# A decoder block's conv norm: the first pair of statistics in split parts in blocks two to four

## The chip, the core and the metric

The kernel runs on one core of a Trainium2 chip. Times are microseconds (us) of device time for one execution of the whole program. The engines of the core are PE (TensorE: matmuls), PEld (its weight load), DVE (VectorE), ACT (ScalarE), POOL (GpSimd) and SP (SyncE, which issues DMAs). Each has its own queue of instructions, executes it in order, and waits on semaphores where it needs another engine's result.

## The reference, cut to what matters

One layer over 2048 tokens of 1024 features: a norm, one input projection, a gated linear attention over half of the columns and a convolution over the other half, an output projection, an MLP, and a last norm. The change is in the norm that follows the convolution:

```python
def channel_group_norm(u, g, b):
    B, S, C = u.shape                                   # C = 512, CONV_GROUPS = 8
    uf = u.astype(jnp.float32).reshape(B, S, CONV_GROUPS, C // CONV_GROUPS)
    mu = jnp.mean(uf, axis=-1, keepdims=True)
    var = jnp.mean(jnp.square(uf - mu), axis=-1, keepdims=True)
    y = ((uf - mu) * lax.rsqrt(var + EPS)).reshape(B, S, C)
    return (y * g.astype(jnp.float32) + b.astype(jnp.float32)).astype(u.dtype)
...
        u = c_in * jax.nn.sigmoid(c_gate)
        u = causal_depthwise_conv(u, conv_w[l], conv_b[l])
        o_conv = jax.nn.silu(channel_group_norm(u, conv_norm_g[l], conv_norm_b[l]))
        mixed = jnp.concatenate([o_gla, o_conv], axis=-1)
        h = h + jnp.einsum('bse,ed->bsd', mixed, w_out[l])
```

## The kernel before

The tokens go through the mixer in four blocks of 512 (`b` = 0 to 3 in the code, blocks 1 to 4 in this text), up to about 700 us of the span; the MLP fills the rest. In a block, the channels of the convolution are four tiles of 128 channels by 512 tokens, `j` = 0 to 3, held in `y_sb`. They are normed in two pairs. The products of the block are made of three fp32r matmuls each, high and low parts of both operands (`three_products`, lines 83 to 85 by their place: L83, L84, L85); twelve such matmuls are one unit of weights.

**The norm's statistics are matmuls.** A 128x128 matrix with 1/64 in two squares, `mean_grp`, averages over the channels of a group. For the second pair (`j` = 2, 3) the operand is split: ACT rounds it to an fp32r high part, `mix_hi` (L1614 for the mean, L1605 for the squares), POOL subtracts it from the operand for the low part, `mix_lo` (L1168 and L1178; DVE in block 4), and PE adds two fp32r matmuls, L2270 on the high part and L2271 on the low part. For the first pair (`j` = 0, 1) PE multiplies the fp32 operand itself: L2585 for the mean, on `y_sb`, and L2595 for the variance, on the squares in `res_sb`. The trace shows each such fp32 matmul as two records, so a pair is one row of four. `mix_hi` and `mix_lo` can't serve the first pair, since they still hold the operands of the block's output projection at that time.

**The steps of the norm** are, for a pair: `cn_mean` (PE the means; DVE takes them from `y_sb`, L2215; ACT squares into `res_sb`, L1603), `cn_var` (PE the variances, ACT their logarithm, L1618), `cn_rstd` (ACT Exp, L1623, POOL the product with `y_sb`, L1183) and, later, `cn_silu` and `cn_mixed` (ACT L1627, and the parts for the output projection, ACT L1636 and POOL L1187).

**What stands around them.** A step `g` is a column of the gate's projection, one or two units of PE (L83 to L85) and ACT's `silu_g` (L1549). The attention works in chunks of 128 tokens: `gla_expo` (DVE L2174 to L2176, then ACT L1567 to L1569 for `fac`), `gla_factors` (POOL: `k_end`, `q_in`, `qk`, L1044 to L1046), `gla_decayed` (POOL: `ke` and `qe` for seven levels, L1158 and L1159), `gla_heads` (ACT copies `qe` into `qe_head`, L1579), `gla_scores` (PE L2617 and L2624 on `qe_head` and `ke`, L2635, L2638), `gla_select` (DVE takes the levels from the scores into `probs`, L2054, L2064) and `gla_out`. `gn_mixed` is POOL's share of the norm of the attention's result of the block before (L1196, L1199), after ACT's `mix_hi` (L1663). `gate` is a small product for the decays (PE L2494, DVE `cum`).

**What sets the order** is one table, `ORDER`, of steps with their block. Each engine walks the whole table and issues its own share of each step in that order:

```python
        def run(do):
            for b, *step in ORDER:
                do(step, b)
```

So a step's place in the table sets its place in all five queues at once; the semaphores alone say how far one engine runs ahead of another. Nothing is reordered later.

## Time and profile before

| | us |
|---|---|
| median of 3 runs | 2025.48 (2025.23 to 2025.58) |
| the profiled execution, its own time | 2025.3 |
| its span | 2023.6 |
| PE busy | 2001.7 (99%) |
| DVE busy | 1474.7 (73%) |
| ACT busy | 957.9 (47%) |
| POOL busy | 443.5 (22%) |

The profile is of one execution; 1.7 us of its time lie outside the span. "Busy" is time in which an engine executes; for PE the ends of matmuls are modelled and overlap the next one's start, so PE's pace is read from the distance of starts. A wait belongs to the instruction that stands at the head of its engine's queue, and the name behind the arrow is the one that ended last by the profile.

### The profile page before, as it was taken

Reading aid. Unit: us, or ns where it says so; the run is one execution under the profiler, and the core shown is the slowest. Engines: PE = TensorE matmul, PEld = TensorE weight load, DVE = VectorE, ACT = ScalarE, POOL = GpSimd, SP = SyncE. Lnnn points to the kernel's source line nnn. Section 1 sums busy time; section 2 is a strip of 40 time slices with the busy share of each in tenths; the row PEclk is TensorE's granted clock in tenths of the full one; section 3 lists DMA queues with packets and bytes.
Section 4 is the critical chain, followed back from the end, with each engine's and each line's share of the span. In section 5 each row is a group of like instructions: output and inputs, shape, how many; then the busy total and the mean of one; then the engine's idle time right before and its main releaser. Section 6 shows DMA issues by size and latency. Waiting matters only on the chain.

```text
span 2023.6 us, 27171 instructions
## 1 busy us (share of the span) xinstructions
PE 2001.7 (99%) x9898; PEld 1636.7 (81%) x9898; DVE 1474.7 (73%) x2178; ACT 957.9 (47%) x1362; POOL 443.5 (22%) x593
## 2 busy tenths in 40 slices
PE   8999999999999999999999999999999999999998
PEld 7787778787878778888888888888888888888887
DVE  3899978887878978877789777777664646545475
ACT  4456664355244563565657554555232333323253
POOL 5543475235126441000000000000020201202031
PEclk9999999999999999999999999999999999999999
DMA  6885458455565555444446433335977567565674
GB/s 229 284 282 158 135 204 295 165 170 183 198 202 198 175 204 194 161 146 141 146 165 210 151 121 124 130 119 193 371 238 265 191 203 262 181 220 186 206 240 176
DMA packets 175268, 395.76 MB, mean 196 GB/s; under 512 B 15424, under 2 KB 64672, under 8 KB 174624
## 3 DMA queue, kind: packets, MB, share of 16 engines
q1 hardware_dynamic: 154688, 317.47, 46.4%
q10 hardware_dynamic: 20448, 76.56, 10.9%
q8 instruction: 79, 1.29, 0.3%
q14 instruction: 53, 0.43, 0.1%
HBM read 301.70 MB, written 92.27 MB: 195 GB/s over the span
## 4 chain that ended last, share of the span: by engine, by line
PE 59%; DVE 0%; issue 0%; POOLq 0%; ACT 0%; POOL 0%; ACTq 0%
PE acc L83 20%; PE acc L85 19%; PE acc L84 19%; PE acc L2331 0%; DVE rows_b L2023 0%; DVE rows_b L2005 0%; DVE f_tile L1895 0%; DVE part_t L1891 0%; DVE ring_sum L1868 0%; POOLq L260 0%; ACT m_junk L1465 0%; POOL m_rstd L1117 0%; ACTq L1470 0%
## 5 line engine op out<-in xcount | busy, mean ns | idle before, releaser
L1985 DVE TENSOR_TENSOR down_lo<-down_raw,down_hi 128x1536 fp32r<-128x1536 f32 x112 | 200.5, 1790 | 229.8 <-ACT down_hi L1440 229.8
L83 PE MATMUL acc<-down_hi 128*128 128x512 f32 x896 | 348.5, 389 | 0.0
L84 PE MATMUL acc<-down_lo,down_hi 128*128 128x512 f32 x896 | 348.5, 389 | 0.0
L85 PE MATMUL acc<-down_hi,down_lo 128*128 128x512 f32 x896 | 348.5, 389 | 0.0
L1440 ACT ACTIVATE down_hi<-down_raw 128x1536 fp32r<-128x1536 f32 x112 | 166.7, 1488 | 360.8 <-PE acc L85 188.9
L1723 DVE SCALAR_TENSOR_TENSOR acc<-u_sb,cw_col,acc 128x512 f32<-128x512 f32 x464 | 313.0, 748 | 0.3
L1354 ACT ACTIVATE ring_hi<-ring_sum 128x512 fp32r<-128x512 f32 x155 | 97.8, 631 | 251.3 <-DVE ring_sum L1868 248.8
L83 PE MATMUL acc<-xT_hi,wt 128*128 128x512 f32 x512 | 204.1, 399 | 1.8 <-DVE u_sb L2088 1.0
L1099 POOL TENSOR_TENSOR rows_a<-rows_a,second 128x512 f32<-128x512 f32 x20 | 25.3, 1300 | 803.5 <-ACT second L1448 655.5
L85 PE MATMUL acc<-xT_hi,wt 128*128 128x512 f32 x512 | 199.7, 390 | 0.0
L84 PE MATMUL acc<-xT_lo,wt 128*128 128x512 f32 x512 | 199.3, 389 | 0.0
L85 PEld LDWEIGHTS acc<-down_hi,down_lo 128*128 128x128 f32 x896 | 168.2, 188 | 35.0
L83 PEld LDWEIGHTS acc<-down_hi 128*128 128x128 f32 x896 | 168.2, 188 | 34.9
L84 PEld LDWEIGHTS acc<-down_lo,down_hi 128*128 128x128 f32 x896 | 168.2, 188 | 34.9
L1868 DVE TENSOR_TENSOR ring_sum<-raw_w 128x512 f32<-128x512 f32 x155 | 108.3, 699 | 65.5 <-PE acc L85 64.2
L83 PE MATMUL acc<-mul_hi,ring_hi 128*128 128x512 f32 x372 | 145.6, 391 | 0.8 <-issue 0.4
L85 PE MATMUL acc<-mul_hi,ring_lo 128*128 128x512 f32 x372 | 144.8, 389 | 0.0
L84 PE MATMUL acc<-mul_lo,ring_hi 128*128 128x512 f32 x372 | 144.8, 389 | 0.0
L1877 DVE TENSOR_TENSOR ring_lo<-ring_sum,ring_hi 128x512 fp32r<-128x512 f32 x155 | 107.4, 693 | 18.4 <-ACT ring_hi L1354 3.8
L83 PEld LDWEIGHTS acc<-xT_hi,wt 128*128 128x128 f32 x512 | 96.2, 188 | 24.1 <-DVE u_sb L2088 1.5
L84 PEld LDWEIGHTS acc<-xT_lo,wt 128*128 128x128 f32 x512 | 96.2, 188 | 20.7 <-issue 1.4
L85 PEld LDWEIGHTS acc<-xT_hi,wt 128*128 128x128 f32 x512 | 96.1, 188 | 20.5
(304 smaller groups left out, 4116.7 us busy)
## 6 DMA issues: line engine op xcount, KB each, us to landing
wt<-w_kept SPq DMA_DIRECT2D x168, 512.0 KB, 3.3
down_raw<-f_kept ACTq DMA_DIRECT2D x109, 512.0 KB, 4.3
raw_w<-in_w_mlp_in SPq DMA_DIRECT2D x32, 1024.0 KB, 6.0
f_kept<-f_tile SPq DMA_DIRECT2D x128, 256.0 KB, 2.0
down_raw<-in_w_mlp_out SPq DMA_DIRECT2D x64, 512.0 KB, 3.7
w_kept<-wt SPq DMA_DIRECT2D x48, 512.0 KB, 5.4
down_raw<-in_w_mlp_out SPq DMA_DIRECT2D x64, 256.0 KB, 3.3
down_more<-f_kept ACTq DMA_DIRECT2D x29, 512.0 KB, 5.4
```

The costliest lines, as they stand in the source:

```text
L83: nc.tensor.matmul(out, w_hi, x_hi, start=first, stop=False, skip_group_check=onto)
L84: nc.tensor.matmul(out, w_hi, x_lo, start=False, stop=False, skip_group_check=onto)
L85: return nc.tensor.matmul(out, w_lo, x_hi, start=False, stop=last, skip_group_check=onto)
L1099: nc.gpsimd.tensor_tensor(into, into, second[:, n, :], op).then_inc(d_add2, 1)
L1354: nc.scalar.activation(blocks(ring_hi[:, j % RING, :]), src, ACT.Copy).then_inc(a_hi, 1)
L1440: nc.scalar.activation(down_hi[d % RING][:, :], down_raw[d % DOWN_RAW][:, 512:2048], ACT.Copy).then_inc(d_hi, 1)
L1723: nc.vector.scalar_tensor_tensor(out=y_sb[:, j, :] if k == TAPS - 1 else bank, in0=u_sb[:, j, k:k + BLK], scalar=cw_col[:, j, k:k + 1], in ...
L1868: nc.vector.tensor_tensor(blocks(ring_sum[:, j % RING, :]), w1_block(w, a), w1_block(w, b), op).then_inc(a_sum, 1)
L1877: nc.vector.tensor_tensor(blocks(ring_lo[:, slot, :]), src, blocks(ring_hi[:, slot, :].bitcast(F32)), ALU.subtract).then_inc(a_lo, 1)
L1985: nc.vector.tensor_tensor(down_lo[slot][:, :], down_raw[d % DOWN_RAW][:, 512:], down_hi[slot][:, :].bitcast(F32), ALU.subtract).then_inc(d ...
```

## The change

In blocks 2 to 4 the first pair's statistics are made of parts too, one tile at a time. A new step `cn_halves(square, j)` lets ACT write the high part of `y_sb` (square = 0) or of its square (square = 1) into `cn_hi0`, and POOL the low part into `cn_lo0`; a new step `cn_of_halves(square, j)` lets PE add the two fp32r matmuls. There is one `cn_hi0` and one `cn_lo0`, laid over the buffer `sig`, so ACT may write the next tile's high part only when PE has read the last one. The squares of `res_sb` are still written (L1603), for the low part. In these blocks `cn_mean` and `cn_var` of the first pair have no matmul left. Block 1 keeps the fp32 matmuls. The second pair's steps are as before, with a new count of the shared semaphores. Three further waits keep other users of `sig` back.

```diff
         z_parts = over("sig", "z_parts", [P, BLK], F32R, 4 * BLK)
+        cn_hi0 = over("sig", "cn_hi0", [P, BLK], F32R)
+        cn_lo0 = over("sig", "cn_lo0", [P, BLK], F32R, 4 * BLK)
...
                 if p == 1:
                     pool.wait_ge(cum_ok, NB * PAIRS * TT)
+                    pool.wait_ge(cn_var_pe, NB * CT)
...
+                elif name == "cn_halves":
+                    square, j = step[1:]
+                    pool.wait_ge(cn_part_hi, cn_parts(b, j, square) + 1)
+                    nc.gpsimd.tensor_tensor(cn_lo0[:, :], cn_work(j) if square else y_sb[:, j, :],
+                                            cn_hi0[:, :].bitcast(F32), ALU.subtract).then_inc(cn_part_lo, 1)
...
                     elif not first(m):
                         act.wait_ge(cum_ok, m * PAIRS * TT)
+                        if b > 0:
+                            act.wait_ge(cn_var_pe, b * CT + 2)
...
+                elif name == "cn_halves":
+                    square, j = step[1:]
+                    if square:
+                        act.wait_ge(cn_dev, b * CT + j + 1)
+                        if j == 0:
+                            act.wait_ge(cn_mean_pe, b * CT + 2)
+                        else:
+                            act.wait_ge(cn_var_pe, b * CT + 1)
+                    elif j == 0:
+                        act.wait_ge(tap_ok, b * ALL_TAPS + PAIR_TAPS)
+                        act.wait_ge(cum_ok, (b + 1) * PAIRS * TT)
+                        act.wait_ge(gate_pe, (b + 1) * PAIRS)
+                    else:
+                        act.wait_ge(cn_mean_pe, b * CT + 1)
+                    nc.scalar.activation(cn_hi0[:, :], y_sb[:, j, :], ACT.Square if square else ACT.Copy).then_inc(cn_part_hi, 1)
                 elif name == "cn_split":
+                    act.wait_ge(cn_var_pe, b * CT + 2)
...
+                elif name == "cn_of_halves":
+                    square, j = step[1:]
+                    if not square and j == 0:
+                        pe.wait_ge(v_ok, (b + 1) * TT)
+                    elif square:
+                        pe.wait_ge(cn_dev, b * CT + j + 1)
+                    pe.wait_ge(cn_part_lo, cn_parts(b, j, square) + 1)
+                    out = acc[:, cn_bank(b, j), :]
+                    nc.tensor.matmul(out, mean_grp_r[:, :], cn_hi0[:, :], start=True, stop=False)
+                    nc.tensor.matmul(out, mean_grp_r[:, :], cn_lo0[:, :], start=False,
+                                     stop=True).then_inc(cn_var_pe if square else cn_mean_pe, 1)
+                elif name in ("cn_mean", "cn_var") and step[1] == 0 and not first(b):
+                    pass
```

The table is written anew. Two of its lines in block 2 (`b` = 1):

```diff
-    (0, "cn_mixed", 1), (1, "gla_scores", 0, 0), (1, "taps", 0, 38, 24), (1, "taps", 1, 0, 1),
-    (1, "gla_select", 0, 0), (1, "cn_mean", 0), (1, "gla_decayed", 1, 0), (1, "g_a", 1), (1, "gla_scores", 0, 1),
+    (0, "cn_mixed", 1), (1, "gla_scores", 0, 0), (1, "gla_scores", 0, 1), (1, "taps", 0, 38, 24),
+    (1, "taps", 1, 0, 1), (1, "gla_select", 0, 0), (1, "cn_halves", 0, 0), (1, "g_a", 1), (1, "cn_of_halves", 0, 0),
+    (1, "cn_halves", 0, 1), (1, "gla_select", 0, 1), (1, "gla_expo", 1), (1, "gla_factors", 1),
```

In block 2, `gla_scores(0, 1)` thus moves ahead of the unit that stands before the first tile, and on POOL nothing new stands before the first low part but what stood before the factors. Elsewhere a few steps swap places: in block 1 `x_norm` 1 and `cn_mean` 0 come somewhat earlier and `x_sq` 2 and `gla_scores(1, 0)` later, and between blocks 1 and 2 `(1, gate, 0)` moves ahead of `(0, gla_scores, 3, 0)`. In the MLP `store` and `back` trade places with a neighbour.

**PE in block 3.** The rows below stand behind the unit before `gla_scores(0, 1)`; `cn_hi_50` and `cn_lo_51` are the two new buffers, `w_again3` is the next unit of weights. Before:

```order
L85 MATMUL acc<-xT_hi,wt 128x512
L2624 MATMUL acc<-qe_head,ke 64x64 [waits probs_ok]
L2624 MATMUL acc<-qe_head,ke 64x64 x15
L2595 MATMUL acc<-res_sb,mean_grp 128x512 [waits cn_sq,cn_dev]
L2595 MATMUL acc<-res_sb,mean_grp 128x512 [waits cn_sq]
L83 MATMUL acc<-xT_hi,wt 128x512 [waits w_again3]
```

and after:

```order
L85 MATMUL acc<-xT_hi,wt 128x512
L2616 MATMUL acc<-cn_hi_50,mean_grp_r 128x512 [waits cn_part_lo,v_ok]
L2617 MATMUL acc<-cn_lo_51,mean_grp_r 128x512
L2672 MATMUL acc<-qe_head,ke 64x64 [waits probs_ok]
L2672 MATMUL acc<-qe_head,ke 64x64 x15
L2616 MATMUL acc<-cn_hi_50,mean_grp_r 128x512 [waits cn_part_lo]
L2617 MATMUL acc<-cn_lo_51,mean_grp_r 128x512
L83 MATMUL acc<-xT_hi,wt 128x512 [waits w_again3]
```

The variance stood behind `gla_scores(0, 1)` (the two rows on `qe_head`); now the mean's first tile stands ahead of it and its second tile behind it, and nothing else is between the two. The fp32 mean stood 24 unit matmuls further up.

**POOL in block 3.** The same stretch of POOL's queue, from the second pair's `y_sb` products of the block before. Before:

```order
L1183 TENSOR_TENSOR y_sb<-y_sb,res_sb 128x512 [waits cn_rs] x2
L1196 TENSOR_TENSOR o_sb<-o_sb,silu_g 128x512 [waits gn_n]
L1199 TENSOR_TENSOR mix_lo<-o_sb,mix_hi 128x512 [waits gn_hi]
L1196 TENSOR_TENSOR o_sb<-o_sb,silu_g 128x512 [waits gn_n]
L1199 TENSOR_TENSOR mix_lo<-o_sb,mix_hi 128x512 [waits gn_hi] x2
L1183 TENSOR_TENSOR y_sb<-y_sb,res_sb 128x512 [waits cn_rs] x2
L1044 TENSOR_TENSOR k_end<-k_sb,fac 128x256 [waits qe_ok,kT_pe,o_pe,score_pe,fac_ok]
```

and after:

```order
L1202 TENSOR_TENSOR y_sb<-y_sb,res_sb 128x512 [waits cn_rs] x2
L1215 TENSOR_TENSOR o_sb<-o_sb,silu_g 128x512 [waits gn_n]
L1218 TENSOR_TENSOR mix_lo<-o_sb,mix_hi 128x512 [waits gn_hi]
L1215 TENSOR_TENSOR o_sb<-o_sb,silu_g 128x512 [waits gn_n]
L1218 TENSOR_TENSOR mix_lo<-o_sb,mix_hi 128x512 [waits gn_hi] x2
L1187 TENSOR_TENSOR cn_lo_51<-y_sb,cn_hi_50 128x512 [waits cn_part_hi] x2
L1057 TENSOR_TENSOR k_end<-k_sb,fac 128x256 [waits qe_ok,kT_pe,o_pe,score_pe,fac_ok]
```

The two low parts of the mean stand behind the last `mix_lo` of `gn_mixed` and ahead of `k_end`; the products with the first pair's own `res_sb` (the second L1183 row) move further down.

**POOL in block 4**, behind the last `mix_lo` of `gn_mixed`. Before:

```order
L1199 TENSOR_TENSOR mix_lo<-o_sb,mix_hi 128x512 [waits gn_hi] x2
L1044 TENSOR_TENSOR k_end<-k_sb,fac 128x256 [waits qe_ok,kT_pe,o_pe,score_pe,fac_ok]
L1045 TENSOR_TENSOR q_in<-q_sb,fac 128x256
L1046 TENSOR_TENSOR qk<-q_sb,k_sb 128x256
L1158 TENSOR_TENSOR ke<-k_sb,fac 128x2x64
L1159 TENSOR_TENSOR qe<-q_sb,fac 128x128
```

and after:

```order
L1218 TENSOR_TENSOR mix_lo<-o_sb,mix_hi 128x512 [waits gn_hi] x2
L1187 TENSOR_TENSOR cn_lo_51<-y_sb,cn_hi_50 128x512 [waits cn_part_hi] x2
L1187 TENSOR_TENSOR cn_lo_51<-res_sb,cn_hi_50 128x512 [waits cn_part_hi]
L1057 TENSOR_TENSOR k_end<-k_sb,fac 128x256 [waits qe_ok,kT_pe,o_pe,score_pe,fac_ok]
L1058 TENSOR_TENSOR q_in<-q_sb,fac 128x256
L1059 TENSOR_TENSOR qk<-q_sb,k_sb 128x256
L1172 TENSOR_TENSOR ke<-k_sb,fac 128x2x64
L1173 TENSOR_TENSOR qe<-q_sb,fac 128x128
L1187 TENSOR_TENSOR cn_lo_51<-res_sb,cn_hi_50 128x512 [waits cn_part_hi]
L1172 TENSOR_TENSOR ke<-k_sb,fac 128x4x32
```

Three low parts stand ahead of chunk 1's `k_end`, and the fourth stands between the first and the second of its seven `ke`, `qe` pairs.

## Rows read from the trace of the kernel before

**Rows 1.** The page: busy time of the engines, granted clock in 40 slices
```profile
PE 2001.7 (99%) x9898; PEld 1636.7 (81%) x9898; DVE 1474.7 (73%) x2178; ACT 957.9 (47%) x1362; POOL 443.5 (22%) x593
...
PEclk9999999999999999999999999999999999999999
```

**Rows 2.** The waits of PE: releaser, us in total, times, longest
```profile
PE acc L2494 <- DVE cum L2110: 1.4, 2, 0.8
PE acc L83 <- DVE u_sb L2088: 1.0, 1, 1.0
...
PE acc L83 <- ACT q_sb L1533: 0.8, 1, 0.8
```

**Rows 3.** The time line (start us, us), PE, block 2, first pair
```profile
264.56 1.88 PE L2585 MATMUL acc<-y_sb,mean_grp 128*128 128x512 f32 x4
...
266.51 0.40 PE L84 MATMUL acc<-xT_lo,wt 128*128 128x512 f32 x1
```

**Rows 4.** The time line, PE, block 1, second pair in parts
```profile
195.15 0.40 PE L2270 MATMUL acc<-mix_hi,mean_grp_r 128*128 128x512 f32 x1
...
196.09 0.39 PE L2485 MATMUL acc<-xT_hi,wz 128*32 128x512 f32 x1
```

**Rows 5.** Groups by line and shape, ACT and POOL: busy us, mean ns
```profile
L1614 ACT ACTIVATE mix_hi<-y_sb 128x512 fp32r<-128x512 f32 x8 | 4.6, 622 | 12.4 <-DVE y_sb L1723 12.4
...
L1168 POOL TENSOR_TENSOR mix_lo<-y_sb,mix_hi 128x512 fp32r<-128x512 f32 x6 | 7.6, 1298 | 44.4 <-ACT mix_hi L1614 44.4
```

**Rows 6.** The time line, POOL and ACT, block 2, around the first pair
```profile
262.87 2.55 POOL L1199 TENSOR_TENSOR mix_lo<-o_sb,mix_hi 128x512 fp32r<-128x512 f32 x2
266.12 2.55 POOL L1187 TENSOR_TENSOR mix_lo<-y_sb,mix_hi 128x512 fp32r<-128x512 f32 x2 [0.70 <-ACT mix_hi L1636]
...
271.92 1.90 ACT L1568 ACTIVATE fac<-fac 128x2048 f32<-128x2048 f32 x1
```

**Rows 7.** The time line, PE, block 3, around the first pair
```profile
450.60 1.88 PE L2585 MATMUL acc<-y_sb,mean_grp 128*128 128x512 f32 x4
...
457.86 1.15 PE L2624 MATMUL acc<-qe_head,ke 128*64 128x64 f32 x32
458.94 1.98 PE L2595 MATMUL acc<-res_sb,mean_grp 128*128 128x512 f32 x4
```

**Rows 8.** The time line, ACT and POOL, block 3, around the first pair
```profile
445.75 1.28 ACT L1543 ACTIVATE v_sb<-acc 128x512 f32<-128x512 f32 x2
448.02 0.39 ACT L1585 ACTIVATE k_endT<-acc 128x256 f32<-128x256 f32 x1 [1.00 <-PE acc L2638]
...
449.14 2.52 POOL L1183 TENSOR_TENSOR y_sb<-y_sb,res_sb 128x512 f32<-128x512 f32 x2 [5.92 <-ACT res_sb L1623]
...
453.11 1.29 POOL L1199 TENSOR_TENSOR mix_lo<-o_sb,mix_hi 128x512 fp32r<-128x512 f32 x1 [0.19 <-ACT mix_hi L1663]
...
456.94 2.57 POOL L1199 TENSOR_TENSOR mix_lo<-o_sb,mix_hi 128x512 fp32r<-128x512 f32 x2 [1.29 <-ACT mix_hi L1663]
```

**Rows 9.** The time line, POOL, ACT, PE, block 4, chunk 1 to its scores
```profile
651.08 0.73 POOL L1044 TENSOR_TENSOR k_end<-k_sb,fac 128x256 f32<-128x256 f32 x1
...
658.77 0.51 POOL L1159 TENSOR_TENSOR qe<-q_sb,fac 128x128 f32<-128x128 f32 x1
...
665.18 1.92 ACT L1579 ACTIVATE qe_head<-qe 64x896 f32<-64x896 f32 x2
...
657.54 1.88 PE L2595 MATMUL acc<-res_sb,mean_grp 128*128 128x512 f32 x4
...
667.15 0.54 PE L2617 MATMUL acc<-qe_head,ke 128*64 128x128 f32 x3
```

**Rows 10.** The time line, DVE, block 2, beside POOL and after it
```profile
265.62 0.69 DVE L2215 TENSOR_TENSOR y_sb<-y_sb,acc 128x512 f32<-128x512 f32 x1 [0.46 <-PE acc L2585]
...
267.42 1.40 DVE L2174 TENSOR_TENSOR fac<-cum 128x128 f32<-128x128 f32 x1
268.74 0.28 DVE L2175 TENSOR_TENSOR fac<-cum 128x128 f32<-128x128 f32 x1
```

More of the change, by code:

```diff
@@ new lines @@
+    (1, "gla_scores", 1, 1), (1, "out", 0, 5), (1, "gla_factors", 2), (1, "out_done", 0, 31),
+    (1, "gla_decayed", 2, 0), (1, "out", 0, 6), (1, "out", 0, 7), (1, "x_tr", 2), (1, "x_tr", 3), (1, "res_load", 1),
+    (1, "taps", 1, 14, 11), (1, "gla_out", 1), (1, "gla_decayed", 2, 1), (1, "gla_select", 2, 0),
+    (1, "gla_decayed", 2, 2), (1, "taps", 1, 25, 3), (1, "gla_expo", 3), (1, "out", 1, 0), (1, "gla_heads", 2),
+    (1, "out", 1, 1), (1, "out", 1, 2), (1, "gla_scores", 2, 0), (1, "out", 1, 3), (1, "gla_select", 2, 1),
@@ L177 @@
+    (2, "x_tr", 1), (2, "gla_decayed", 1, 2), (2, "x_sq", 2), (2, "gla_heads", 1), (2, "taps", 1, 14, 3),
+    (2, "gla_out", 0), (2, "taps", 1, 17, 7), (2, "gla_expo", 2), (2, "out", 0, 0), (2, "out", 0, 1),
+    (2, "res_load", 0), (2, "out", 0, 2), (2, "out", 0, 3), (2, "gla_select", 1, 0), (2, "x_sq", 3),
     (2, "gla_scores", 1, 0), (2, "out", 0, 4), (2, "out", 0, 5), (2, "gla_factors", 2), (2, "gla_select", 1, 1),
@@ new lines @@
+    (3, "out_done", 1, 39), (3, "gla_out", 3), (3, "taps", 1, 61, 1), (3, "gn_square"), (3, "cn_split", 1),
+    (3, "up0_part", 0, 2), (3, "gn_sum", 0), (3, "up0_part", 2, 3), (3, "cn_mean", 1), (4, "x_norm", 1),
+    (3, "up0_part", 3, 4), (4, "x_tr", 0), (3, "gn_sum", 1), (3, "gn_mixed", 0), (3, "up0_part", 4, 8),
+    (3, "gn_rstd"), (3, "gn_mixed", 1), (3, "cn_var", 1), (3, "up0", 1), (4, "x_tr", 1), (4, "m_load", 1),
+    (4, "out", 0, 0), (4, "x_norm", 2), (3, "gn_mixed", 2), (4, "out", 0, 1), (4, "out", 0, 2), (3, "cn_rstd", 1),
```

185 lines of the change are left out of this document (89 added, 96 removed).

## The prediction

> **What bounds the kernel now.** I read the page first: PE is busy for 99% of the span at the full granted clock, and the other engines have room, POOL most of all at 22% [rows 1]. Then the waits of PE. They are few. Those that touch the change are two short ones between blocks 1 and 2, for `cum` and for `q_sb`, and one of 1.0 us at 188 us, in block 1, for DVE's `u_sb` [rows 2]; around the first pairs of blocks 2 to 4 it doesn't wait at all. So a microsecond taken from PE's queue is a microsecond of the end, as long as nothing makes PE stand, and every new wait of PE is a full loss. Last I read the time lines of PE, ACT and POOL at the first pair of each block, to see who would be late for the new matmuls. The reader is to see there that PE's queue is dense and that POOL, idle on average, is busy in a row just where the pair stands.
>
> **What is removed and what PE gets instead.** In block 2 the fp32 pair starts at 264.56; the second unit matmul behind it starts at 266.51, the first thus at about 266.28, since two neighbours start 0.227 us apart. A pair holds PE 1.72 us [rows 3]. Six pairs go: 6 x 1.72 = 10.3. Four matmuls on high and low parts took 196.09 - 195.15 = 0.94, or 0.47 for one tile [rows 4]; twelve tiles come: 12 x 0.47 = 5.6. **Term 1: -4.7 us.** The bounds are near, -4.5 and -4.9, because both kinds stand in the trace.
>
> **What ACT and POOL get.** Twelve high parts of 0.62 us on ACT and twelve low parts of 1.3 us on POOL [rows 5]; two POOL instructions in a row take 2.55, so 1.25 to 1.28 from start to start [rows 6]. (The Trainium skill, page "Perfetto Trace Analysis", section "GPSIMD Engine Instruction", says that a GpSimd span is unreliable and that the distance of starts should be taken; the trace has both, and they differ by 0.04.) 7.5 and 15 us on engines at 47% and 22% cost nothing by themselves. What counts is that each tile is now a chain in front of PE: PE's last reading of the buffers, ACT 0.63, POOL 1.28, PE. With the 0.39 until the last tile's record ends and some 0.15 for the hand-overs that is 2.45 us from tile to tile with one buffer pair, against 12 unit matmuls = 2.72 where a unit stands between. That just hides it. So I go through the places where less stands between, or where POOL is not free.
>
> **Block 2, first mean tile.** PE would be there at 264.56 + 1.15 for `gla_scores(0, 1)` (the size of its row in block 3 [rows 7]) + 2.72 = 268.4. POOL works without a gap up to 265.4, and then, ahead of the low part by the table, the two `mix_lo` of the second pair from 266.12 to 268.6 [rows 6]; the low part ends at 269.9. **+1.45.** The wait of `gla_scores(0, 1)` for its `probs`, which stands nearer now, lies inside this, since PE would meet the same POOL anyway.
>
> **Block 3, first mean tile.** PE: 450.60 + 24 unit matmuls = 456.0 [rows 7]. POOL: seven instructions stand ahead of the low part, from the products with `res_sb` at 449.14 to the last `mix_lo`. These products can start 1.5 earlier, behind `v_sb` at 447.0 and ACT's Exp, as `k_endT` no longer stands before that; the short idle times of 0.19 and 1.29 between them go too, their `mix_hi` being earlier in ACT's queue [rows 8]. 447.7 + 7 x 1.26 = 456.5, and with two hand-overs and the low part 457.9. **+1.9.**
>
> **Block 3, second mean tile.** Only `gla_scores(0, 1)` stands between the two tiles, 1.15 and the 0.2 of the matmul itself, under a chain of 2.45. **+1.2**, whatever POOL does before.
>
> **Block 4, `gla_scores(1, 0)`.** Call S the time at which PE may begin the first variance tile; POOL starts `k_end` then, since three low parts stand ahead of it. From `k_end` to the last `qe` POOL took 651.08 to 659.3 = 8.2; with the fourth low part 1.28 and ACT's `qe_head` 1.92 the scores may start at S + 11.4. PE needed 667.15 - 657.54 = 9.6 from the fp32 variance to the scores; minus 1.8 for the pair, plus 0.94 it is there at S + 8.75 [rows 9]. **+2.6.** Before, POOL was done 6 us before ACT took up `qe_head`: that cover is what the three low parts use up. `x_tr` and the output projection are queued behind the scores on PE and can't fill the time.
>
> **Four weaker waits.** From the second mean tile to the first variance tile the chain is longer: record 0.39, DVE's subtraction 0.69 [rows 10], two ACT passes 1.25, POOL 1.28, hand-overs 0.2 = 3.8. In block 4 a unit and the tile's own time, 3.0, cover it: 0.8. In blocks 2 and 3 two units do, but in ACT's queue the exponential of `fac`, 1.90 with its table loads, stands ahead of the squares [rows 6]: 0.8 and 0.6. In block 2 two weight parts of 1.28 stand on POOL ahead of the last low part: 0.5. Together 2.7; each is a difference of two long sums with an error as large as itself, so I take half, 1.35, and keep 0 and 2.7 for the range.
>
> **Moves between blocks 1 and 2.** `(1, gate, 0)` is issued earlier, so the 0.80 for `cum` goes, and PE meets `q_sb` a little later relative to ACT. I take -1.0, with bounds 0 and -1.6 (both waits whole [rows 2]). In block 1 the moves change nothing: DVE's convolution taps set when `u_sb` is there at 188 us, and PE waits for it before and after. The swaps in the MLP I cost at nothing, between -0.3 and +0.3, since PE's rows are the same ones there. The three added waits for `sig`: the sigmoid, `cn_split` and a sum in the MLP stand over 10 us behind the last variance tile; none.
>
> **The sum.** 2025.3 (the profiled execution) - 4.7 - 1.0 + (1.45 + 1.9 + 1.2 + 2.6 = 7.15) + 1.35 = 2028.1. The profiled execution is 0.2 under the median of the runs, so 2028.3, 2.8 us above the kernel before: 0.14%, under the 0.2% (4.1 us) that a measurement of this kernel can tell from no change. With the bounds of the terms this case alone spans 2026 to 2029.5 and a little more.
>
> **Rival 1: the waits are hidden and the gain shows.** If POOL is through earlier than I count (its queue slips forward once ACT's order changes) only the tile pair without a unit between them costs, 1.2: 2025.5 - 5.7 + 1.2 = 2021.0, and 2019.8 without that. For it speaks that POOL's waits in the trace are mostly for ACT, and ACT's steps move forward; against it, that in blocks 2 and 3 POOL has no gap left to close. It takes stalls of under 1.6 us in all to be faster by more than 0.2%.
>
> **Rival 2, slower: the hand-overs.** Twelve times a result goes PE, ACT, POOL, PE, and my 0.15 for three of them comes from gaps of 0.05 to 0.1 between ACT and DVE or POOL. No row shows PE waiting for POOL in the mixer, the last hand-over. If a round costs 0.3 more, the 0.27 of slack behind each unit is gone and nearly each of the twelve tiles adds 0.3: +3.6 less what half of the weak ones hold already, 2028.3 + 3.3 = 2031.6. It decides from 0.1 more per tile: then 2029.5.
>
> **Rival 3, slower: DVE and POOL in each other's way.** Two equal DVE subtractions took 1.40 beside a POOL instruction and 0.28 after it [rows 10]. The kernel's sum holds no price for that. Twelve more POOL instructions may each hold up one DVE instruction by 1.1; in block 4, where DVE works without a gap, three in a row delay `probs` and `fac` by 3.3, of which 2.6 is waited for anyway, and in blocks 2 and 3 each first variance tile comes 1.1 later: 0.7 + 2.2, 2031.2. Against it: most of DVE's work there is convolution taps with one operand in `acc`, and these keep their pace beside POOL. The Trainium skill (page "SBUF — State Buffer", section "SBUF: two separate sides") has this as a rule: an exclusive lock between GpSimd and a DVE instruction with two SBUF operands. The trace agrees with it, at 1.40 against 0.28.
>
> **Rival 4: the parts don't save.** If the new matmuls took an fp32 tile's time the sum would lack term 1: 2033. Rows 4 speak clearly against it.
>
> **How the numbers follow.** My case 0.46 (0.04 of it beyond 2029.5), rival 1 0.23 (0.17 under 2021.4, the rest above), rival 2 0.20, rival 3 0.09, rival 4 0.02. Faster: 0.17. Slower: 0.04 + 0.20 + 0.09 + 0.02 = 0.35, less 0.02 of rival 2 that stays under 2029.5 = 0.33. Same: 0.50. The range goes from 2020.8 (rival 1 with its structural wait) to 2031.8 (rivals 2 and 3) and leaves out less than 2 in 10.
>
> **What would show it.** In the new trace: PE waits for the low part on POOL at the first matmul of a tile, about 1.5 in block 2, 1.9 and 1.2 in block 3, and for `qe_head` in block 4 about 2.6; no wait for `cum` at the start of block 2; PE's start distances of 0.23 over the new matmuls. If the waits on the low part are absent, POOL's start of the first low part in blocks 2 and 3 tells where I was late. If they appear at all twelve tiles, rival 2 holds. If DVE's L2174 or its subtraction is stretched in front of a wait, it is rival 3. I would be wrong most plainly if the end moved by something in the MLP.

## The result, and the profile after

| | before, us | after, us |
|---|---|---|
| median of 6 runs | 2025.61 (2025.23 to 2026.39) | 2034.11 (2033.21 to 2035.68) |
| ratio, 95% interval | 1 | 1.0042 (1.0031 to 1.0053) |
| the profiled execution, its own time | 2025.3 | 2033.2 |
| its span | 2023.6 | 2031.5 |

The changed kernel is slower by 8.5 us. The forecast, 2028.3 with a range to 2031.8, was too low. The profiled execution is the fastest of the changed kernel's six, 0.9 us under their median; what follows explains its 7.9 us. The two pages look alike; the rows of the page that answer to [rows 1], of after:

```profile
PE 2002.2 (99%) x9898; PEld 1639.4 (81%) x9898; DVE 1477.2 (73%) x2178; ACT 967.0 (48%) x1376; POOL 460.2 (23%) x605
...
PEclk9999999999999999999999999999999999999999
```

PE executes as many matmuls as before (12 fp32 ones became 24 shorter ones, each fp32 one being two records of the trace) and is "busy" for as long, although the parts should have saved it 4.7 us. In slices of 51 us the clock looks full. Neither says where 8 us are. The waits of PE do (engine, line, releaser: us in total, times, longest), to be set beside [rows 2]:

```profile
PE acc L2616 <- POOL cn_lo L1187: 4.2, 5, 2.0
PE acc L2665 <- ACT qe_head L1600: 2.2, 1, 2.2
...
PE acc L2320 <- ACT silu_g L1570: 1.7, 2, 0.9
...
PE acc L2672 <- DVE probs L2101: 1.2, 2, 1.0
PE acc L83 <- POOL wt L1030: 1.2, 1, 1.2
PE acc L83 <- ACT q_sb L1554: 1.1, 1, 1.1
```

The waits for `cum` are gone, and so is the one of 1.0 for `u_sb` in block 1; `q_sb` went from 0.8 to 1.1. New are five waits for the low part, the one for `qe_head`, one of 1.0 for `probs`, one of 1.2 for weight parts (`wt`) at 112 us in block 1, and two for `silu_g`. The prediction names neither the last three nor the end of the wait for `u_sb`.

**A ledger by blocks.** To see where the end moves, I matched PE's matmuls of the two traces by line and order and took the difference of their starts. Its growth over a stretch is that stretch's shift:

| profiled execution of after against before | shift, us |
|---|---|
| start, block 1 and the passage to block 2 | -0.96 |
| block 2 | +2.20 |
| block 3 | +3.88 |
| block 4 | +3.19 |
| MLP | -0.43 |
| end | +7.9 |

All kernels of this document but the first share the table up to block 2, and yet their first row of this ledger goes from -0.13 to -2.18 from one profiled execution to the next; in blocks 2 to 4 they differ by about 0.1 where neither rows nor clock differ. So the shifts of these blocks are the sharpest measure that follows, and the first row is a weak one.

Block 2 in PE's time line (start us, us, ... [idle before <- releaser]):

```profile
264.79 1.15 PE L2672 MATMUL acc<-qe_head,ke 128*64 128x64 f32 x32 [1.03 <-DVE probs L2101]
...
278.23 0.39 PE L85 MATMUL acc<-xT_hi,wt 128*128 128x512 f32 x1
279.04 0.47 PE L2616 MATMUL acc<-cn_hi,mean_grp_r 128*128 128x512 f32 x1 [0.42 <-POOL cn_lo L1187]
...
282.78 0.47 PE L2616 MATMUL acc<-cn_hi,mean_grp_r 128*128 128x512 f32 x1 [0.29 <-POOL cn_lo L1187]
...
287.85 1.06 PE L2320 MATMUL acc<-ident,x_nat 128*128 128x128 f32 x8 [0.77 <-ACT silu_g L1570]
```

One thing is to be read with care here. The idle time in brackets counts from the modelled end of the matmul before, and that lies 0.39 behind its start, while matmuls that wait for nothing start 0.23 apart. From 278.23 to 279.04 PE stood 0.58, not 0.42, and the first part behind a wait takes 0.07 longer than one that waits for nothing. Each wait of the table costs 0.2 to 0.25 more than it shows.

Block 3, PE's time line:

```profile
459.46 0.64 PE L2616 MATMUL acc<-cn_hi,mean_grp_r 128*128 128x512 f32 x1 [2.02 <-POOL cn_lo L1187]
459.90 0.63 PE L2617 MATMUL acc<-cn_lo,mean_grp_r 128*128 128x512 f32 x1
460.46 1.98 PE L2672 MATMUL acc<-qe_head,ke 128*64 128x64 f32 x32
463.21 0.50 PE L2616 MATMUL acc<-cn_hi,mean_grp_r 128*128 128x512 f32 x1 [0.77 <-POOL cn_lo L1187]
...
480.47 1.07 PE L2320 MATMUL acc<-ident,x_nat 128*128 128x128 f32 x8 [0.89 <-ACT silu_g L1570]
```

The same stretch in windows (from:to, us, PE busy (matmuls), granted clock, DMA share, GB/s):

```profile
459.00:460.00 1.00, 0.54 (x2) 0.80 0.94 385
460.00:461.00 1.00, 1.00 (x12) 0.50 0.07 25
...
462.00:463.00 1.00, 0.44 (x10) 0.50 0.00 0
463.00:464.00 1.00, 0.79 (x3) 1.00 0.00 0
```

Behind the stand of 2.02 us the clock falls to half, its lower level of 1.2 GHz, for 3.4 us (the two half-full slices counted by their share): the 32 small matmuls of `gla_scores` take 1.98 instead of 1.15 [rows 7]. The same happens in block 4, behind the wait for `qe_head`:

```profile
674.05 0.54 PE L2665 MATMUL acc<-qe_head,ke 128*64 128x128 f32 x3 [2.20 <-ACT qe_head L1600]
...
676.25 2.80 PE L2320 MATMUL acc<-ident,x_nat 128*128 128x128 f32 x16
679.62 0.47 PE L2601 MATMUL acc<-wt,mix_hi 128*128 128x512 f32 x1 [0.58 <-issue]
```

Its windows:

```profile
675.00:676.00 1.00, 1.00 (x18) 0.50 0.00 0
676.00:677.00 1.00, 1.00 (x6) 0.50 0.00 0
```

From the scores to the output projection PE needs 5.57 where it needed 671.32 - 667.15 = 4.17 before: 1.4 more behind the wait.

Why the parts are late in block 3 stands in the time lines of POOL and DVE of after. POOL:

```profile
455.46 2.59 POOL L1218 TENSOR_TENSOR mix_lo<-o_sb,mix_hi 128x512 fp32r<-128x512 f32 x2
458.01 1.30 POOL L1187 TENSOR_TENSOR cn_lo<-y_sb,cn_hi 128x512 fp32r<-128x512 f32 x1
461.27 1.88 POOL L1187 TENSOR_TENSOR cn_lo<-y_sb,cn_hi 128x512 fp32r<-128x512 f32 x1 [1.96 <-ACT cn_hi L1642]
```

DVE, the chain of subtractions that makes the factors:

```profile
455.52 1.39 DVE L2211 TENSOR_TENSOR fac<-cum 128x128 f32<-128x128 f32 x1
...
458.12 1.34 DVE L2211 TENSOR_TENSOR fac<-cum 128x128 f32<-128x128 f32 x1
459.39 0.28 DVE L2212 TENSOR_TENSOR fac<-cum 128x128 f32<-128x128 f32 x1
...
461.61 0.41 DVE L2213 TENSOR_TENSOR fac<-cum 128x256 f32<-128x256 f32 x1
```

Each of three POOL instructions holds up one of DVE's subtractions (1.34 to 1.39 for 0.28). Then it turns round: DVE's remaining twelve run without a gap to 462.02; the second low part is taken up at 461.27 and ends at 463.15, 1.13 behind the last of them, where a free one takes 1.28 in all. The rows fit this: it stood until DVE's row was through. The Trainium skill has this rule (page "SBUF — State Buffer", section "SBUF: two separate sides"): whichever of the two starts first keeps the shared port pair for its whole instruction, and the other one blocks. The trace agrees for single instructions, both ways (1.34 for 0.28 on DVE, 1.88 for 1.28 on POOL). That a row of twelve separate DVE instructions lets POOL in nowhere is more than the rule says; the rows alone show it.

### The profile page after: what moved, and what is told of

It reads as the page before. It is cut to its first block, busy times and chain, and to the rows that moved or that the text cites. A ratio compares the mean times of both kernels' runs of the same rounds, so it can differ in the third digit from the quotient of the medians.

```text
span 2031.5 us, 27209 instructions
## 1 busy us (share of the span) xinstructions
PE 2002.2 (99%) x9898; PEld 1639.4 (81%) x9898; DVE 1477.2 (73%) x2178; ACT 967.0 (48%) x1376; POOL 460.2 (23%) x605
## 4 chain that ended last, share of the span: by engine, by line
PE 90%; DVE 3%; ACT 3%; issue 2%; POOL 1%; DMA 0%; DVEq 0%; ACTq 0%; POOLq 0%
PE acc L83 24%; PE acc L85 24%; PE acc L84 24%; PE acc L2601 3%; PE acc L2603 3%; PE acc L2602 3%; PE acc L2672 1%; PE acc L2555 1%; PE acc L2556 1%; PE acc L2557 1%; PE acc L2320 1%; ACT ring_hi L1373 1%; PE acc L2707 1%; DVE ring_sum L1905 1%; DVE acc L1760 0%
```

## The experiments

Each kernel is compared with the kernel before on the same chip (medians 2025.3 to 2025.6 there). Theory A of the first runs is that a tile's way through ACT and POOL, and POOL's longer queue, make PE stand, and that the moves in the table cost little; the rivals are that the moves, the hand-overs, the buffer, the lower clock or the shared port are the cost. "Shift" is a block's shift against the kernel before, as in the ledger.

**The table without the parts.** e1 keeps after's table, leaves out what `cn_halves` does on ACT and POOL, and puts the fp32 matmul of a tile where the parts were:

```diff
                 elif name == "cn_halves":
                     square, j = step[1:]
-                    pool.wait_ge(cn_part_hi, cn_parts(b, j, square) + 1)
-                    nc.gpsimd.tensor_tensor(cn_lo0[:, :], cn_work(j) if square else y_sb[:, j, :],
-                                            cn_hi0[:, :].bitcast(F32), ALU.subtract).then_inc(cn_part_lo, 1)
...
                 elif name == "cn_of_halves":
-                    nc.tensor.matmul(out, mean_grp_r[:, :], cn_hi0[:, :], start=True, stop=False)
-                    nc.tensor.matmul(out, mean_grp_r[:, :], cn_lo0[:, :], start=False,
+                    nc.tensor.matmul(out, mean_grp[:, :], cn_work(j) if square else y_sb[:, j, :], start=True,
```

> The changed kernel's table with the fp32 matmuls back at the places of the new steps, and no high or low parts for the first pair on ACT and POOL. Theory A (the added time is the chain PE, ACT, POOL, PE of each tile and POOL's longer queue, the table's moves cost little): no wait for a low part, none of 2.2 us for qe_head, the granted clock stays up; the wait for probs in block 2 (1.03) stays, the 1.0 gained before block 2 stays, the 4.7 of the fp32 matmuls come back: 2025 to 2027.5. Rival B (the table's moves cost the time): 2031 or more.

Measured: 2027.03 us, ratio 1.0005 (0.9996 to 1.0014). Shifts: block 2 +2.20, block 3 +0.70, block 4 +0.33. PE's waits in this kernel:

```profile
PE acc L2298 <- ACT silu_g L1563: 1.4, 2, 0.8
PE acc L2652 <- DVE probs L2079: 1.2, 2, 1.0
```

No tile waits here, and yet block 2 loses exactly what it loses in after. The time lies in theory A's range, but the moves aren't free: the table alone brings the waits for `probs` and `silu_g`, and costs 1.4 in the profiled execution. In block 2 the parts' waits just eat what the parts save.

**The parts without POOL.** e2 leaves out the low parts and their matmuls (the statistics are then made of the high parts alone); a tile waits for ACT only:

```diff
-                    pe.wait_ge(cn_part_lo, cn_parts(b, j, square) + 1)
+                    pe.wait_ge(cn_part_hi, cn_parts(b, j, square) + 1)
...
-                    nc.tensor.matmul(out, mean_grp_r[:, :], cn_hi0[:, :], start=True, stop=False)
-                    nc.tensor.matmul(out, mean_grp_r[:, :], cn_lo0[:, :], start=False,
+                    nc.tensor.matmul(out, mean_grp_r[:, :], cn_hi0[:, :], start=True,
```

> POOL's twelve low parts and PE's matmuls on them are left out (the first pair's statistics in blocks 2 to 4 are those of the high parts alone); ACT's high parts, the buffer and the table stay. Theory A with POOL as the late one: the waits on the first pair's parts go (4.2), the 2.2 for qe_head and the low clock behind the two long waits (2 to 2.5) go as well, and 12 matmuls (2.8): 2034.1 - 11.5 = 2022.6, 2021 to 2024.5. Rival C (ACT's high part alone, through the one buffer, is what PE waits for): only the 12 matmuls go, 2031.

Measured: 2021.65, ratio 0.9979 (0.9969 to 0.9988). Shifts +0.21, -0.59, -1.60. This is theory A's range again. 2.8 us of the gain are only the twelve matmuls left out (12 x 0.23); set back, this would be 2024.4. What is left between that and 2034.1, 9.7 us, is what it costs that each tile passes over POOL, with the half clock that comes of it. Still there are `probs` (1.02) and `silu_g` (0.84 and 1.18), and `qe_head` with 0.82.

**Work in the place of the stands.** e3 puts nine matmuls of no use ahead of block 3's first mean tile and ahead of block 4's `gla_scores(1, 0)`, so that PE works there instead of standing. e6 adds eight ahead of block 3's second mean tile:

```diff
+                    for _ in range((9, 8)[j] if b == 2 and not square else 0):
+                        nc.tensor.matmul(acc[:, cn_bank(b, j), :], mean_grp_r[:, :], xT_hi[:, 0, :], start=True, stop=True)
                     pe.wait_ge(cn_part_lo, cn_parts(b, j, square) + 1)
...
                     c, part = step[1:]
+                    if b == NB - 1 and c == 1 and part == 0:
+                        pe.wait_ge(probs_ok, (b * TT + c) * SELECTS + SCORE_LEVELS[part][0])
+                        pe.wait_ge(o_ok, b * TT + c)
+                        for _ in range(9):
+                            nc.tensor.matmul(acc[:, S_BANK, :], mean_grp_r[:, :], xT_hi[:, 0, :], start=True, stop=True)
```

The lines are those of e6.

> Nine matmuls of 128x512 whose result nobody reads are added on PE just ahead of the two longest waits, block 3's first mean tile and block 4's scores of chunk 1, so that PE works (2.0 us each) where it stood for 2.0 and 2.2. Theory D (the granted clock falls to its lower level because PE stood that long, and costs 0.8 to 1.2 and 1.4 us on top of the waits): the clock stays up at both places, 2034.1 - 2.3 = 2031.8, 2031 to 2032.7. Rival E (the clock falls there for another reason, or costs nothing since the next wait takes it up): 2033.8 to 2034.8.

Measured: 2033.45, ratio 1.0035 (1.0022 to 1.0048), between the ranges of the two theories, with five executions from 2031.2 to 2034.9. Shifts 2.23, 5.46, 2.34. In block 4 the clock stays full and the shift is 0.85 smaller. In block 3 the second tile now waits 2.03 us, at full clock, and the fall stands behind that wait instead. The time line of PE in e3:

```profile
464.06 0.51 PE L2618 MATMUL acc<-cn_hi,mean_grp_r 128*128 128x512 f32 x1 [2.03 <-POOL cn_lo L1187]
```

And its windows:

```profile
464.00:465.00 1.00, 0.94 (x4) 0.92 0.00 0
...
467.00:468.00 1.00, 1.00 (x4) 0.50 0.00 0
468.00:469.00 1.00, 1.00 (x6) 0.87 0.00 0
```

The units behind it run at half speed, and that costs 1.6 more than the half clock cost in after, where it fell on work that had to wait for the second low part anyway.

> As in the run with matmuls nobody reads, and eight more of them ahead of block 3's second mean tile, where PE stood for 2.0 there and the clock fell behind it. Theory D (the clock falls behind a stand of about 2 us, and no other cause): it stays up in all of blocks 3 and 4; against the run with filler at two places 1 to 1.5 less, 2032.2, 2031.3 to 2033, and a profile without any stretch at the lower level there. Rival E (something else takes the clock down around block 3's mean): a fall is still there and the time is 2033.4 or more.

Measured: 2032.23, ratio 1.0029 (1.0018 to 1.004), in theory D's range. Shifts 2.23, 3.91, 2.31; the clock is full throughout blocks 3 and 4. So the half clock explains 0.9 in block 4 (3.19 against 2.31). In block 3 it explains nothing of the profiled execution (3.88 against 3.91). From the first to the second tile it takes 3.75 in after, 3.84 in e3 and 3.86 in e6, at half clock, at full clock and with work between: it is POOL's second low part that sets it, and that again waits for DVE's row. POOL in e6:

```profile
460.64 2.34 POOL L1187 TENSOR_TENSOR cn_lo<-y_sb,cn_hi 128x512 fp32r<-128x512 f32 x1 [1.53 <-ACT cn_hi L1642]
```

It ends at 462.98, and DVE's row of subtractions in e6 at 461.82. The filler itself holds PE in the same place, so e6 bounds what the clock costs and can't show a gain.

**Chunk 1's factors earlier in block 4.** e4 moves `gla_decayed(1, *)`, which carries POOL's `k_end` to `qe`, ahead of the low parts; of the table's lines:

```diff
-    (3, "gla_scores", 0, 1), (3, "g_a", 1), (3, "g", 1), (3, "cn_of_halves", 0, 0), (3, "cn_halves", 0, 1),
-    (3, "taps", 1, 9, 2), (3, "gla_select", 0, 3), (3, "g_a", 2), (3, "cn_of_halves", 0, 1), (3, "cn_mean", 0),
+    (3, "gla_scores", 0, 1), (3, "gla_decayed", 1, 0), (3, "g_a", 1), (3, "g", 1), (3, "cn_of_halves", 0, 0), (3, "cn_halves", 0, 1),
+    (3, "gla_decayed", 1, 1), (3, "taps", 1, 9, 2), (3, "gla_select", 0, 3), (3, "g_a", 2), (3, "cn_of_halves", 0, 1), (3, "cn_mean", 0),
```

> In block 4 alone chunk 1's k_end, q_in, qk and the seven pairs of ke and qe are put between the low parts on POOL instead of behind the third: the first part of them after the first low part, the rest after the second and the third. Theory F (the 2.2 us wait for qe_head and the low clock behind it come from that order on POOL): both go, 2034.1 - 3.4 = 2030.7, 2029.8 to 2031.7. Rival G (the low parts then come late by as much, the work on POOL is only moved): 2033.3 to 2034.8.

Measured: 2030.51, ratio 1.0024 (1.0015 to 1.0034), in theory F's range. Block 4's shift goes from 3.19 to 0.10: the wait for `qe_head` shrinks from 2.20 to 0.51, the half clock goes, and nothing as large takes their place. This settles block 4: POOL's queue was the cause, by the three low parts ahead of `k_end`. Block 3, whose rows are the same as after's, shifts by 5.64 in this execution. The windows of e4 tell why:

```profile
459.00:460.00 1.00, 1.00 (x24) 0.55 0.00 0
...
465.00:466.00 1.00, 1.00 (x4) 0.53 0.00 0
466.00:467.00 1.00, 1.00 (x6) 1.00 0.00 0
```

Behind the same wait (2.04 us) it stays at half for 6.8 us instead of 3.4, and slows the second tile and the unit behind it too: 1.76 us more. The price of one and the same stand thus differs from execution to execution. This fits the spread of after's runs, 2.5 us where before's is 1.2, but doesn't prove it: beside the experiments single executions of the kernel before reached 2029.5.

**Two buffer pairs.** e5 gives tile 1 buffers of its own (`cn_hi1` in the other half of `sig`, the low parts in unused rows of `res_sb`), so that ACT need not wait for PE's last reading:

```diff
-                    else:
-                        act.wait_ge(cn_mean_pe, b * CT + 1)
-                    nc.scalar.activation(cn_hi0[:, :], y_sb[:, j, :], ACT.Square if square else ACT.Copy).then_inc(cn_part_hi, 1)
+                    nc.scalar.activation(cn_his[j][:, :], y_sb[:, j, :], ACT.Square if square else ACT.Copy).then_inc(cn_part_hi, 1)
```

> The changed kernel's table, with two buffer pairs instead of one: the high parts in the two halves of sig, each low part in its tile's place in res_sb, so that a tile's parts no longer wait for PE to read those of the tile before. Theory H (the wait of 0.8 to 1.3 at block 3's second mean tile and much of what the low clock costs there come from the one buffer pair): that wait goes, the first one of 2.0 stays, 2034.1 - 2 = 2032, 2031 to 2033. Rival I (POOL is the late one for both tiles, the buffer is not what binds): 2033.5 to 2035.

Measured: 2034.38, ratio 1.004 (1.0027 to 1.0053), in rival I's range. Shifts 2.76, 4.52, 3.20. The second mean tile of block 3 no longer waits, and the first variance tile does. PE in e5:

```profile
470.35 0.47 PE L2615 MATMUL acc<-cn_hi,mean_grp_r 128*128 128x512 f32 x1 [0.97 <-POOL cn_lo L1192]
```

DVE in e5:

```profile
459.85 1.36 DVE L2211 TENSOR_TENSOR fac<-cum 128x128 f32<-128x128 f32 x1
461.13 0.28 DVE L2210 TENSOR_TENSOR fac<-cum 128x128 f32<-128x128 f32 x1
```

The second low part, now right behind the first, holds up a fourth subtraction. The row starts 0.4 later than in after and ends 1.6 later (463.57 against 462.02), and behind it come ACT's exponential of `fac` and then the squares. The single buffer was a place where the wait showed, not its cause.

**Own orders for blocks 2 to 4.** e7 takes e4's block 4, puts `gla_scores(0, 1)` of block 2 back behind the unit, as in the kernel before, and in block 4 moves `gla_heads` ahead of the variance's logarithm on ACT. e8 takes that, e5's buffers, and in block 3 both low parts of the mean ahead of the first pair's `gn_mixed` products:

```diff
-    (1, "gn_mixed", 2), (2, "g_a", 0), (1, "gn_mixed", 3), (2, "gla_scores", 0, 0), (2, "g", 0), (2, "taps", 1, 1, 4),
-    (2, "gla_expo", 1), (2, "cn_halves", 0, 0), (2, "g_a", 1), (2, "cn_of_halves", 0, 0), (2, "cn_halves", 0, 1),
+    (2, "cn_halves", 0, 0), (2, "cn_halves", 0, 1), (1, "gn_mixed", 2), (2, "g_a", 0), (1, "gn_mixed", 3), (2, "gla_scores", 0, 0), (2, "g", 0), (2, "taps", 1, 1, 4),
+    (2, "gla_expo", 1), (2, "g_a", 1), (2, "cn_of_halves", 0, 0),
```

> As the run with chunk 1's factors early in block 4, and two moves more: in block 2 gla_scores(0, 1) stands behind the unit again instead of ahead of it, in block 4 gla_heads stands ahead of the variance's logarithm on ACT. If the 1.03 wait for probs in block 2 and the 0.5 left for qe_head come from these places: 2030.5 - 1.2 = 2029.3, 2028.6 to 2029.9. If POOL's first low part in block 2 takes up what the first move frees (by the sum of the prediction it does, 1.45 in all): 2030.

Measured: 2031.25, ratio 1.0023 (1.0013 to 1.0032), above both forecasts, and e4's time within the intervals: no gain. Block 4's shift is 0.01, with no wait for `qe_head` left; block 2's is 2.21, as in after: the wait for `probs` goes, and the first tile waits 1.43 us for POOL. One stands behind the other, as the prediction had it.

> Two buffer pairs, both moves of the run before and block 4's early factors, and in block 3 the high and low parts of both mean tiles ahead of gn_mixed 2 and 3, so that POOL makes them before the last five instructions of the attention's norm instead of behind them. Theory A in full (the time is lost to POOL's order and the buffer, not to the parts themselves): block 3 loses its waits of 2.0 and 0.8 to 1.3 and the low clock, 2029.3 - 5.3 = 2024, 2022.5 to 2025.3. Rival J (gn_mixed or silu_g, now later, make PE wait in their turn): 2026 or more.

Measured: 2035.49, ratio 1.0042 (1.0028 to 1.0056), over 10 us above theory A's range: rival J holds. Block 3 shifts by 8.47. The mean's two tiles wait no more, but what was pushed back collides with DVE's row as a whole. POOL in e8:

```profile
456.11 4.43 POOL L1220 TENSOR_TENSOR o_sb<-o_sb,silu_g 128x512 f32<-128x512 f32 x1
```

One product of 1.3 us stands 3.1 us; ACT's `mix_hi`, `silu_g` and `fac` are queued behind it, PE waits 1.49 for `silu_g` and 4.92 for the first variance part. Of all trials this is the largest single price of the shared port.

**The low parts on DVE.** e9 moves them from POOL to DVE (two operands in SBUF, with e5's buffers), table as in after. e10 has a table for it: PE does both tiles of a pair behind each other, the mean's parts are made earlier (in block 3 ahead of `gn_mixed`), the variance's matmuls stand later in blocks 2 and 4, and `gla_scores(0, 1)` and `gla_heads` stand as in e7. Of e9's edit:

```diff
-                    nc.gpsimd.tensor_tensor(cn_lo0[:, :], cn_work(j) if square else y_sb[:, j, :],
+                    nc.vector.tensor_tensor(cn_los[j][:, :], cn_work(j) if square else y_sb[:, j, :],
```

> The run with two buffer pairs, and the twelve low parts made by DVE (0.69 us each) instead of POOL (1.28), at the same places of the table. Theory K (POOL's queue is what makes the parts late, whatever is done about the buffers): the 2.0 ahead of block 3's first tile and the 2.2 for qe_head in block 4 go with the low clock behind them, though DVE now stands for the high parts inside its own order, which should give back 2 to 3: 2034.4 - 8.5 + 2.5 = 2028.5, 2026 to 2031. Rival L (the table places the steps so that any engine is late): 2033 or more.

Measured: 2044.51, ratio 1.0097 (1.0081 to 1.0112), the slowest of all and rival L's case. In block 2 DVE's queue holds `cn_lo` ahead of `probs`, and PE waits 5.27 for these; in block 3 it waits 4.28 and 3.66 for `cn_lo` itself. From the waits of PE in e9:

```profile
PE acc L2673 <- DVE probs L2093: 5.5, 2, 5.3
```

> As the run with the low parts on DVE, with the steps moved so that both tiles' parts are made together where DVE and ACT have time and PE does both tiles in a row: in block 2 behind gla_select(0, 1), in block 3 behind cn_silu 1 with five taps ahead, in block 4 behind x_norm 0; the squares' parts ahead of the next silu_g. Theory K: no wait for a part, none for qe_head, full clock: per block -1.57 against the kernel before in blocks 3 and 4, about -0.6 in block 2, -0.7 between blocks 1 and 2: 2025.5 - 4.4 = 2021.1, 2019.8 to 2022.5, faster than both kernels. Rival M (DVE, standing for the parts, delays the attention's exponents, selections or taps until PE waits for those): 2024 or more.

Measured: 2031.59, ratio 1.0031 (1.002 to 1.0043), 10 us above theory K: rival M holds. Shifts 1.03, 3.90, 3.34. Two stands of nearly 2 us are left, each with half clock behind it. PE's time line in e10:

```profile
465.70 0.47 PE L2618 MATMUL acc<-cn_hi,mean_grp_r 128*128 128x512 f32 x1 [1.94 <-DVE cn_lo L2258]
...
673.75 1.54 PE L2322 MATMUL acc<-ident,x_nat 128*128 128x128 f32 x8 [1.97 <-DVE x_nat L1761]
```

In block 4 the clock is at half for 6.8 us behind it.

**One stand at a time.** e11 moves two steps of e10's table:

```diff
-    (2, "g_a", 2), (2, "taps", 1, 13, 1), (2, "gla_select", 0, 3), (2, "x_load", 2), (2, "cn_of_halves", 1, 0),
-    (2, "cn_of_halves", 1, 1), (2, "g", 2), (2, "gla_decayed", 1, 1), (2, "g_a", 3),
+    (2, "g_a", 2), (2, "taps", 1, 13, 1), (2, "gla_select", 0, 3), (2, "x_load", 2), (2, "g", 2), (2, "cn_of_halves", 1, 0),
+    (2, "cn_of_halves", 1, 1), (2, "gla_decayed", 1, 1), (2, "g_a", 3),
...
-    (2, "cn_silu", 1), (3, "gla_decayed", 1, 2), (3, "gla_expo", 2), (3, "x_norm", 1), (3, "gla_heads", 1), (3, "cn_var", 0),
+    (2, "cn_silu", 1), (3, "gla_decayed", 1, 2), (3, "x_norm", 1), (3, "gla_expo", 2), (3, "gla_heads", 1), (3, "cn_var", 0),
```

> The kernel of e10 (low parts on VectorE, two pairs of buffers, own table) with two moves: in block 3 the two variance tiles of the first pair stand behind the unit g(2) instead of ahead of it (12 unit matmuls later), and in block 4 x_norm(1) stands ahead of the factors of chunk 2 on VectorE instead of behind them. In e10 TensorE waited 1.94 us for the first variance part in block 3 and 1.97 us for x_norm in block 4, and behind both the granted clock stood at about half for some us. Theory 1 (waits of about 2 us cost themselves and a stretch of half clock behind them): both waits go, the clock stays at 1.00 in blocks 3 and 4, block 3 shifts by +0.0 to +1.5 us against the kernel before instead of +3.9, block 4 by -1.5 to +0.5 instead of +3.3, and the whole takes 2021.5 to 2026 us. Theory 2 (what is lost is the work that the engines share, and the waits only show where it surfaces): other waits take their place (chunk 2's scores for the factors that are 1.3 us later in block 4, x_tr for silu_g in block 3), and the time stays over 2029 us.

Measured: 2027.03, ratio 1.0006 (0.9997 to 1.0015), between the two forecasts. Block 3: from +3.90 to -0.77, more than the wait itself; no wait for another engine over 0.7, clock full. Theory 1 holds there. Block 4: +2.49 instead of +3.34. There theory 2 holds: the stand moved on. PE in e11:

```profile
671.20 0.77 PE L2603 MATMUL acc<-wt,mix_hi 128*128 128x512 f32 x1 [3.28 <-issue]
```

"Issue" names no releaser. Two operands came just then: `mix_lo` (POOL from 669.44, first one done about 670.7) and the second `xT_lo` (DVE from 669.82, done about 671.1). e12 moves both forward:

```diff
-    (2, "cn_silu", 1), (3, "gla_decayed", 1, 2), (3, "x_norm", 1), (3, "gla_expo", 2), (3, "gla_heads", 1), (3, "cn_var", 0),
+    (2, "cn_silu", 1), (3, "gla_decayed", 1, 2), (3, "x_norm", 1), (3, "gla_heads", 1), (3, "cn_var", 0),
...
-    (3, "x_tr", 0), (3, "x_tr", 1), (2, "cn_mixed", 1), (3, "x_load", 3), (3, "x_sq", 2), (3, "taps", 1, 20, 1),
+    (3, "x_tr", 0), (2, "cn_mixed", 1), (3, "x_tr", 1), (3, "gla_expo", 2), (3, "x_load", 3), (3, "x_sq", 2), (3, "taps", 1, 20, 1),
```

> The kernel of e11 with two more moves in block 4: on VectorE the factors of chunk 2 (gla_expo(2), 3.3 us) go behind the low halves of x's transposes instead of ahead of them, and on ScalarE the second pair's mix_hi of block 3 stands between the two halves of the transposes instead of behind both. In e11 TensorE reached the output projection of block 4 about 668 us into the span and stood there for 3.28 us (to 671.20), when xT_lo (VectorE from 669.82) and mix_lo (GpSimd from 669.44) came; behind this the granted clock was 0.50 for some 3 us, and a lead of 2.64 us over the kernel before turned into a lag of 1.41. Theory 1 (the stand and the low clock behind it are all that is lost there): the projection starts at 669.0 to 669.8 us, with little or no stretch of half clock, and the whole takes 2022.5 to 2024.5 us, less than the kernel before. Theory 2 (the lag only surfaces there, and what waits on the factors of chunk 2 is as late as before): TensorE waits for the key and query factors of chunk 2 instead, and the time stays at 2026 to 2028 us.

Measured: 2024.8 (2023.84 to 2025.8, 11 runs), ratio 0.9996 (0.9987 to 1.0005). Block 4's shift is 0.59, and the clock stays full there. Time and start of the projection lie just above theory 1's ranges. PE in e12:

```profile
669.91 0.47 PE L2603 MATMUL acc<-wt,mix_hi 128*128 128x512 f32 x1 [0.88 <-issue]
```

So PE's queue with the parts in it can be fed without the loss, with the low parts off POOL and three waits taken out one by one. But the best of it can't be told from the kernel before. What the parts save, 4.6, went elsewhere; waits for `silu_g` of 0.61, 0.82 and 0.66 are among it, and the rest isn't taken apart here. The profiled execution of e12 is the slowest of its eleven.

## Where the prediction was right and where not

By its own steps, with the stands taken from the distances of starts:

| term | predicted | measured |
|---|---|---|
| parts instead of fp32 matmuls | -4.7 | -4.6 |
| moves up to block 2 | -1.0 | -0.96 |
| block 2, first tile with `probs` | 1.45 | 1.5 |
| block 3, first tile | 1.9 | 2.2 |
| block 3, second tile | 1.2 | 2.1 |
| block 4, scores wait for `qe_head` | 2.6 | 2.3 |
| the weaker waits, at half | 1.35 | 2.3 |
| `x_tr` waits for `silu_g`, blocks 2 and 3 | 0 | 2.1 |
| block 4 behind the scores | 0 | 1.4 |
| MLP | 0 | -0.4 |
| sum | +2.8 | +7.9 |

**Right** were the places. The tile of parts costs 0.48 where it waits for nothing and an fp32 tile 0.86 (e1). The two heavy waits in block 3 and the one in block 4 came where they were expected, within 0.3 for the first mean tile of blocks 2 and 3 and for `qe_head`; e4 confirms the last by its cause. That `probs` and POOL stand behind each other in block 2 is confirmed by e7. The wait for `cum` went as said.

**Right by luck** was the term for the moves up to block 2. It put block 1 at nothing and had PE wait for `u_sb` before and after; in fact that wait of 1.04 went, and one of 1.16 for `wt` came at 112 us. In two of the thirteen profiled executions with this table, e4's and e6's, the wait for `wt` is missing, and there the kernel is 1.1 us less late from there on. The MLP, put at nothing within 0.3, gave back 0.4.

**Wrong was, first, a missing term:** the sum has nothing for the chain behind a variance tile. `x_tr` in blocks 2 and 3 needs a bank of `acc` that ACT empties with `silu_g`, and in ACT's queue `silu_g` stands behind the variance's logarithm, between two loads of tables. ACT's time line in after, block 2:

```profile
283.23 1.28 ACT L1655 ACT_TABLE_LOAD   x1
284.53 1.27 ACT L1655 ACTIVATE res_sb<-acc,eps_col 128x512 f32<-128x512 f32 x2
285.81 1.28 ACT L1570 ACT_TABLE_LOAD   x1
287.11 0.60 ACT L1570 ACTIVATE silu_g<-acc 128x512 f32<-128x512 f32 x1
```

That is 4.5 us of chain behind the second variance tile. Before, both fp32 tiles stood together at 278.48, with two units between them and `x_tr`; now the second stands one unit further down and only one unit covers the chain. I had followed what waits for a tile's matmul ahead of PE, but not what hangs on its result. e1 shows this without any part: 0.84 and 0.52.

**Second, the weak waits were taken at half.** Their full sum was 2.7; measured are 0.65, 0.1, 0.9 and 0.5, and 0.2 for block 2's second mean tile, 2.3 in all. Halving small differences that all point one way was a choice against the rows.

**Third, the second mean tile of block 3.** The chain was forecast at 2.45 from the first tile's low part to the second tile, and took 3.31 (459.90 to 463.21). 0.24 of that is the low part's matmul at half clock (0.63 for 0.39), 0.6 is POOL standing behind DVE's row. The forecast took POOL's instruction at its free 1.28. At full clock POOL is there earlier and only stands longer (2.32 in e3, 2.34 in e6), and the tile comes no sooner. Rival 3 had named the port, with POOL in DVE's way. That happened too: the first low part held up one subtraction by 1.06 and with it the whole row. But the price came back on POOL, which the prediction doesn't have.

**Fourth, what a stand costs beyond itself.** In block 4 the scores' wait of 2.2 was followed by 1.4 more. e3 and e6 give the clock 0.85 to 0.9 of it; for the other 0.5 only the rows speak: the projection waits behind ACT's transposes, which are behind `silu_g` and its table load, which are behind `qe_head`. That part isn't shown by an experiment. In block 3 the half clock cost nothing in the profiled execution, since the second low part was late anyway, and 1.8 in e4's.

Rival 2 falls: four of twelve tiles wait for nothing (three in block 4, one in block 3, each 0.23 behind the matmul before), and where they wait a cause stands in POOL's or DVE's queue. But its amount per hand-over, 0.3, is near the 0.2 to 0.25 by which the idle column understates a wait. Rival 4 falls by the first row of the table. What stays open is how much of the 2.5 us spread of after's runs the clock makes, and with it the 0.6 us between the ledger and the medians; the ledger exists for profiled executions only.
